# Sixteen conditioning rows at the start of a decoder kernel: summed by TensorE in column form instead of by VectorE

## The chip, the cores and the metric

The kernel runs on 1 core of one Trainium2 chip. The metric is the device time of one execution in microseconds (us), lower is better.

## The reference, cut to what matters

A two-layer decoder trunk on 256 tokens of width 1024. Every layer is steered by a conditioning vector: `mod = silu(c) @ w_mod + b_mod`, six rows of 1024 numbers a layer. The first two of them, shift and scale, are needed before anything else of the layer can be computed:

```python
c_act = jax.nn.silu(c)
for l in range(DEPTH):
    mod = (c_act @ w_mod[l] + b_mod[l])[:, None, :]
    sh1, sc1, g1, sh2, sc2, g2 = jnp.split(mod, 6, axis=-1)
    h = x * (1.0 + sc1) + sh1
    y = hybrid_mixer(h, w_in[l], ...)          # projections, sparse attention, gated linear attention
    x = layer_norm(DN_ALPHA * x + (1.0 + g1) * y, ...)
    h = x * (1.0 + sc2) + sh2
    y = swiglu(h, ...) if l % 2 == 0 else moe_swiglu(h, ...)
    x = layer_norm(DN_ALPHA * x + (1.0 + g2) * y, ...)
```

All of it is in f32.

## The kernel before

Every engine has its own program, and semaphores tie them together. The DMA queue of SyncE (SP) issues nearly all loads in an order that is written out by hand, and waits in that order too: what stands behind a waiting load waits with it.

The product `c_act @ w_mod[0]` for shift (a = 0) and scale (a = 1) is cut into sixteen blocks of 128 x 1024: block (a, k) holds the 128 input rows k of part a, so a row of the block lies on a partition. `FIRST_ROWS` is the order in which they are loaded: (1,0) to (1,3), then (1,4), (0,0), (1,5), (0,1), (1,6), (0,2), (1,7), (0,3), and last (0,4) to (0,7). The two halves of the tokens x are loaded behind the entries 9 and 11 of that list (`X_AFTER`). Below, block 0 to block 15 are the entries of this list.

VectorE takes each block as it lands, multiplies it by one number per partition (`c_act[:, k]`, silu of c, with the input index on the partitions) and adds it to the sum of its part, `ycat[:, a, :]` (lines 1464 and 1467). When a part is whole (`mod_sum`), TensorE sums over the partitions: `sum_chunk` (lines 1016 to 1019) multiplies eight pieces of 128 columns by a column of ones, so that the sums come out as eight columns, in the form in which VectorE needs them. Each piece is four matmuls of 128 x 32 weights (`mm4`, line 974), and each such f32 matmul is two matmul records and two weight loads in the trace. One part is thus 64 records.

In between, TensorE transposes a bias tile into bank 7 (`stage`, line 1013), waits until VectorE has copied it (`cols_rd`), transposes a second one (`stage2`, line 1024), and transposes the tokens (`transposed_tokens`, line 983: 16 transposes of 128 x 128 into banks 0 to 3). It does this between the sums of the two parts.

The sum of the second part signals `mod_ps`. Then:

- VectorE adds the biases (line 1454, `conditioning`) and modulates the transposed tokens, eight tiles of `hfull` (line 1499).
- TensorE starts unit 0 of the input projection (line 1054: f32, 32 records; a projection unit is 256 columns of `w_in`), then unit 1 (line 1048).
- ScalarE splits later units into a high part (line 679, `u_high`), VectorE makes the low part (line 1550, `u_low`), and TensorE multiplies them (lines 340 to 342). ScalarE's order is: split unit 2, high part of the tokens (line 720), split unit 3, copy the results of units 0 and 1 out (lines 701 and 705), split unit 4.
- SP, which has issued units 0 to 3 without a wait, issues conditioning rows 0 and 1 of the later parts into the buffers of `ycat`, behind `mod_ps` (line 412), then unit 4 behind the end of unit 0's matmuls (`proj`, line 427), for unit 4 takes its buffer. Rows 2 and 3 come next, behind VectorE's work on row 0, then unit 5.
- GpSimd, which had waited for `mod_sum` of both parts, issues the loads of `g_row`, `wa2`, `lng_row`, `lnb_row` and `gnorm` (lines 592 to 610).

The rest of the kernel: attention and gated linear attention of layer 0, a dense SwiGLU, the mixer of layer 1, and from about 540 us on the routed experts, TensorE's longest stretch.

Of the kernel before, what the change touches and what calls it, by code (L numbers as in the profile page):

```python
# [20 lines left out]
ALU = mybir.AluOpType  # L21
# [3 lines left out]
P = 128  # L25
D = 1024
KT = D // P
# [62 lines left out]

FIRST_ROWS = [(1, k) for k in range(4)] + [(a, k + 4 * a) for k in range(4) for a in (1, 0)] + [(0, k) for k in range(4, 8)]
X_AFTER = (9, 11)

HF0, HF1, YC0, YC1, X0 = range(5)
NROWBUF = X0 + 8
# [14 lines left out]
def hybrid_decoder(nc, x, c, w_in, w_a2, b_a, gla_norm_g, w_out, w_mod, b_mod, ln_g, ln_b,  # L110
# [3 lines left out]
    with ctx:  # L114
# [17 lines left out]
        x_sb = place("x_sb", [P, TT, D])  # L132
        hTH_at = top[0]
        hT_H = place("hT_H", [P, KT, T], F32R)
        hTL_at = top[0]
        hT_L = place("hT_L", [P, KT, T], F32R)
        hfull_at = top[0]
        hfull = place("hfull", [P, KT, T])
        ycat_at = top[0]
        ycat = place("ycat", [P, TT, D])  # L140
# [14 lines left out]
        ident = place("ident", [P, P])  # L155
# [5 lines left out]
        stage2 = place("stage2", [P, P])  # L161
        ln_cols = place("ln_cols", [P, 64])
        cols = place("cols", [P, P])
        modT = place("modT", [P, DEPTH * 48])
# [3 lines left out]
        c_act = place("c_act", [P, KT])  # L168
# [90 lines left out]
        mod_first = place("mod_first", [P, KT, 2 * D], at=over)  # L259
# [37 lines left out]
        bank = [ctx.enter_context(nc.psum_tensor(f"bank{i}", [P, 512], F32)) for i in range(8)]  # L297


        s = {}  # L300
        for name in """const c_ld x_ld stage_ld stage2_ld small_ld rows_ld wa2_ld pads stageT cols_rd cact mod_sum ik row_rd mod_ps modT x_ln xT_ps hfull hT_H hT_L
            brow_ld gn_ld wH wL proj evac idx_ps relu idxacc dve_chain act_chain pool_chain z_ps az decay
            qe ke kx_e kfac_rd gla_in hfull_a lnm wo at_ps at_sb at_msk o_ps ssq rms lg_ps lg_sb nmax pexp pt_ps pt_sb pv_ps ycat
            yT_ps yT_H yT_L mv rstd x_n g3 stored
            f_guH f_guL f_gu f_silu f_hid f_t f_tH f_tL f_dH f_dL f_d
            rt_ps lg8 expd sel rank_ps npass lg_rd xb_ps xsplit G xg_ps xg
            zeroed row_to sent x_rows x_turned y_kept y_all row_back came
            m_used m_silu m_hid m_tH m_oS m_st m_S m_sc m_acc m_y0 m_y1 m_end""".split():
            s[name] = sem("s_" + name)
        row_ld = [sem(f"s_row_ld{i}") for i in range(NROWBUF)]  # L310
        mod_ld = row_ld + [sem(f"s_mod_ld{i}") for i in range(NROWBUF, len(FIRST_ROWS))]
# [222 lines left out]
        def _(pool):  # L534
            n = [0]
# [80 lines left out]
                    link(pool.tensor_scalar(rms[:, t, :], ssq[:, t, :], 1.0 / B_DV, EPS, ALU.mult, ALU.add))  # L616
                    pool.tensor_tensor(rms[:, t, :], rms[:, t, :], half_neg[:, 4:8], ALU.pow).then_inc(s["rms"], 1)

            pool.wait_ge(s["mod_sum"], 2)
            gate_bias(0, 2, g_row)  # L620
            mixer(0)
            norm_power(0)
# [344 lines left out]
        def _(pe):  # L967
# [9 lines left out]
            def transposed_tokens(src, signal):  # L977

                for b in range(4):
                    for i in range(2):  # L980
                        for t in range(TT):
                            kt = 2 * b + i
                            last = nc.tensor.transpose(bank[b][:, i * T + t * P:i * T + (t + 1) * P],
                                                       src[:, t, kt * P:(kt + 1) * P], ident[:])
                    last.then_inc(s[signal], 1)
# [29 lines left out]
            def sum_chunk(acc, o):  # L1015

                for k in range(KT):
                    last = mm4(o[:, k:k + 1], acc[:, k * P:(k + 1) * P], ones[:, 0:1], start=True, stop=True)
                return last
            pe.wait_ge(s["mod_sum"], 1)  # L1020
            sum_chunk(ycat[:, 1, :], bank[6][:, KT:2 * KT])
            pe.wait_ge(s["cols_rd"], 1)
            pe.wait_ge(s["stage2_ld"], 32)
            nc.tensor.transpose(bank[7][:, 0:P], stage2[:], ident[:]).then_inc(s["stageT"], 1)
            pe.wait_ge(s["x_ld"], 32)
            transposed_tokens(x_sb, "xT_ps")
            pe.wait_ge(s["mod_sum"], 2)
            sum_chunk(ycat[:, 0, :], bank[6][:, 0:KT]).then_inc(s["mod_ps"], 1)

            def project(l, u, between=None):  # L1030
                b = bank[4 + u % 2]
# [303 lines left out]
            for t in range(TT):  # L1335
                for kt in KT_ORDER:
                    token_tile(3, t, kt)
                    last = mm4(bank[(7, 5)[t]][:, 0:NE], hfull[:, kt, t * P:(t + 1) * P], wr[:, kt, :],
                               start=(kt == KT_ORDER[0]), stop=(kt == KT_ORDER[-1]))
# [88 lines left out]
            for t in range(TT):  # L1428
                for g in range(GROUPS):
                    if t == 0:  # L1430
                        pe.wait_ge(s["m_y1"], n_done + g + 1)
                    for h in range(2):
                        half = slice(64 * h, 64 * h + 64)
                        last = mm(bank[(6, 0)[t] + h][:], last_S[half, g, t * P:(t + 1) * P], y_last[half, g, :],
                                  start=(g == 0), stop=(g == GROUPS - 1))
# [5 lines left out]
        def _(dve):  # L1441
            V = nc.vector
            n = [0]
# [11 lines left out]
                                              in1=cols[:, c0:c0 + 8], op0=ALU.add, op1=ALU.add)  # L1455


            dve.wait_ge(s["cact"], 1)
            before = [0, 0]
            for i, (a, k) in enumerate(FIRST_ROWS):  # L1460
                dve.wait_ge(mod_ld[i], 16)
                w, acc = mod_first[:, k, a * D:(a + 1) * D], ycat[:, a, :]
                if k == 0:
                    last = V.tensor_scalar(acc, w, c_act[:, 0:1], None, ALU.mult)
                else:
                    dve.wait_ge(s["dve_chain"], before[a])
                    last = V.scalar_tensor_tensor(out=acc, in0=w, scalar=c_act[:, k:k + 1], in1=acc,
                                                  op0=ALU.mult, op1=ALU.add)
                if k == KT - 1:
                    last.then_inc(s["mod_sum"], 1)  # L1470
                else:
                    last.then_inc(s["dve_chain"], 1)
                    n[0] += 1
                    before[a] = n[0]
                if i == 8:
                    dve.wait_ge(s["stageT"], 1)
                    V.tensor_copy(cols[:], bank[7][:, 0:P]).then_inc(s["cols_rd"], 1)
            dve.wait_ge(s["cols_rd"], 1)
            dve.wait_ge(s["mod_ps"], 1)
            for a in range(2):  # L1480
                last = conditioning(0, a, bank[6][:, a * KT:(a + 1) * KT])
# [354 lines left out]
            for t in range(TT):  # L1836
                last = V.tensor_tensor(lg[:, t, :], bank[(7, 5)[t]][:, 0:NE], br_row[:], ALU.add)
# [21 lines left out]
            for p in range(1, PASSES):  # L1859
                last = V.tensor_scalar(rank_tab[:, :, 1 + p * NE:1 + (p + 1) * NE], rank_m[:], -1.0 - p * SLOTS, None, ALU.add)  # L1860
# [25 lines left out]
            for p in range(PASSES):  # L1886
                last = V.tensor_tensor(gate_tab[:, :, 1 + p * NE:1 + (p + 1) * NE], gate[:], tmp[:], ALU.add)
# [90 lines left out]
            for t in range(TT):  # L1978
                last = V.tensor_scalar(last_G[:, t].rearrange("p g (q s) -> p g q s", q=4),
                                       slot_id[:, 0:SLOTS].rearrange("p (g s) -> p g s", g=GROUPS).unsqueeze(2).broadcast_to([P, GROUPS, 4, 32]),  # L1980
                                       rank_tab[:, t, bass.ds(n_done, 1)], None, ALU.is_equal)
            last.then_inc(s["m_oS"], 1)
            dve.wait_ge(s["came"], 32 * TT)
            for t in range(TT):
                link(V.tensor_scalar(ycat[:, t, :], back[t][0][:], gate_back[:, 0, t:t + 1], None, ALU.mult))
                link(V.scalar_tensor_tensor(out=ycat[:, t, :], in0=back[t][1][:], scalar=gate_back[:, 1, t:t + 1], in1=ycat[:, t, :],
                                            op0=ALU.mult, op1=ALU.add))
                link(V.tensor_tensor(ycat[:, t, :], ycat[:, t, :], gate3_row[:], ALU.mult))
                link(V.scalar_tensor_tensor(out=ycat[:, t, :], in0=x_sb[:, t, :], scalar=ALPHA, in1=ycat[:, t, :],
                                            op0=ALU.mult, op1=ALU.add))  # L1990
# [4 lines left out]
            for t in range(TT):  # L1995
                accumulate(n_done, (2 * t, 2 * t + 1), ((6, 7), (0, 1))[t])
                dve.wait_ge(s["m_acc"], 2 + 2 * t)
                for h in range(2):
                    last = V.bn_stats(stats[:, t, h, :], ycat[:, t, h * 512:(h + 1) * 512])
# [4 lines left out]
            for t in range(TT):  # L2004
                last = V.scalar_tensor_tensor(out=x_sb[:, t, :], in0=ycat[:, t, :], scalar=mv[:, t, 0:1], in1=lng_row[:],
                                              op0=ALU.subtract, op1=ALU.mult)
# [29 lines left out]
```

## Time and profile before

| | us |
|---|---|
| median of 3 runs | 1260.71 |
| lowest, highest | 1260.42, 1261.34 |
| profiled execution, its own time | 1262.0 |
| its span in the trace | 1260.3 |
| TensorE matmul busy | 1155.7 |
| VectorE busy | 546.0 |
| ScalarE busy | 284.0 |

The span runs from the first instruction to the last; the execution's own time is 1.7 us longer. Busy shares are over the whole span, and stages differ: in the first 125 us VectorE is busy most of the time and TensorE often waits, and in the last 700 us TensorE is nearly always busy.

### The profile page before, as it was taken

The numbers are of one execution on the slowest core, as the hardware profiler recorded it, in microseconds if no ns is written. First come the engines' busy times: TensorE is split into PE (matmuls) and PEld (weight loads), VectorE is DVE, ScalarE is ACT, GpSimd is POOL, SyncE is SP. The second block draws the span as 40 slices with busy tenths as digits, with TensorE's granted clock in tenths as the row PEclk, the third lists the DMA queues.
The fourth block names the chain that finished last, engine by engine and source line by source line (L and its number), as shares of the span: only waits on it lengthen the run. The fifth ranks groups of instructions, "written<-read, shape, count | busy, mean of one in ns | idle before, by whom it ended". The sixth has DMA issues, their size and how long they took to land.

```text
span 1260.3 us, 25818 instructions
## 1 busy us (share of the span) xinstructions
PE 1155.7 (92%) x11004; PEld 634.8 (50%) x11004; DVE 546.0 (43%) x881; ACT 284.0 (23%) x486; POOL 64.9 (5%) x118
## 2 busy tenths in 40 slices
PE   1887979999988899899999999999999999999986
PEld 1876868778867898642333333333333333333322
DVE  6798688867756999842110110121011101110124
ACT  0553524343334656211010010010000100100100
POOL 2102000000202001010000000000000000000101
PEclk9998989999989999899999999999999999999988
DMA  9979496889972955999999999999999999999991
GB/s 341 323 233 278 173 335 210 296 324 385 303 249 67 290 172 177 362 388 338 413 412 398 410 405 404 412 397 412 412 392 411 413 390 410 412 402 411 412 389 56
DMA packets 156504, 422.69 MB, mean 335 GB/s; under 512 B 20988, under 2 KB 74656, under 8 KB 145120
## 3 DMA queue, kind: packets, MB, share of 16 engines
q1 hardware_dynamic: 146720, 395.16, 82.3%
q0 software_dynamic: 6080, 20.31, 5.0%
q10 hardware_dynamic: 3584, 5.51, 1.3%
q8 instruction: 89, 1.46, 0.5%
q14 instruction: 31, 0.25, 0.1%
HBM read 405.20 MB, written 15.73 MB: 334 GB/s over the span
## 4 chain that ended last, share of the span: by engine, by line
PE 67%; DVE 13%; DMA 11%; issue 4%; SPq 3%; ACT 2%; POOL 0%; DVEq 0%; ACTq 0%
PE bank L1372 32%; PE bank L1386 17%; PE bank L340 4%; PE bank L342 4%; PE bank L341 4%; DMA raw_u<-in_ffn_w_up_dram 4%; DVE mod_acc L1539 3%; DMA raw_w<-in_moe_w_down_dram 3%; DVE u_low L1550 2%; DMA raw_w<-in_moe_w_up_dram 2%; DMA u_raw<-in_w_in_dram 1%; PE bank L1260 1%; DMA mod_first<-in_w_mod_dram 1%; SPq L487 1%; ACT gu_H L843 1%
## 5 line engine op out<-in xcount | busy, mean ns | idle before, releaser
L1372 PE MATMUL bank<-raw_w,xg 128*32 128x512 f32 (+1 forms) x4608 | 460.1, 558 | 5.2 <-DMA raw_w<-in_moe_w_up_dram 3.0
L1372 PEld LDWEIGHTS bank<-raw_w,xg 128*32 128x32 f32 x4608 | 154.0, 110 | 308.1 <-issue 300.5
L1924 DVE TENSOR_TENSOR he<-he,bank 128x256 f32<-128x256 f32 (+1 forms) x72 | 25.7, 384 | 533.8 <-ACT he L897 533.8
L1386 PE MATMUL bank<-raw_w,heT 128*32 128x512 f32 x2112 | 232.9, 596 | 3.0 <-DMA raw_w<-in_moe_w_down_dram 2.9
L1386 PEld LDWEIGHTS bank<-raw_w,heT 128*32 128x32 f32 x2112 | 71.9, 110 | 157.7 <-issue 152.9
L897 ACT ACTIVATE he<-bank 128x256 f32<-128x256 f32 (+1 forms) x72 | 21.3, 367 | 571.2 <-PE bank L1372 571.2
L1539 DVE SCALAR_TENSOR_TENSOR mod_acc<-mod_row,c_act,mod_acc 128x1024 f32<-128x1024 f32 x70 | 89.8, 1283 | 9.1 <-DMA mod_row<-in_w_mod_dram 3.2
L340 PE MATMUL bank<-u_high,hT_H 128*128 128x256 f32 x256 | 74.7, 292 | 4.7 <-DVE u_low L1550 3.3
L342 PE MATMUL bank<-u_high,hT_L 128*128 128x256 f32 x256 | 72.1, 282 | 0.0
L341 PE MATMUL bank<-u_low,hT_H 128*128 128x256 f32 x256 | 72.0, 281 | 0.0
L679 ACT ACTIVATE u_high<-u_raw 128x2048 fp32r<-128x2048 f32 x26 | 49.7, 1912 | 69.3 <-DMA u_raw<-in_w_in_dram 43.8
L340 PE MATMUL bank<-gu_H,hT_H 128*128 128x512 f32 x160 | 64.8, 405 | 0.0
L342 PE MATMUL bank<-gu_H,hT_L 128*128 128x512 f32 x160 | 63.2, 395 | 0.0
L341 PE MATMUL bank<-gu_L,hT_H 128*128 128x512 f32 x160 | 63.1, 394 | 0.0
L1550 DVE TENSOR_TENSOR u_low<-u_raw,u_high 128x2048 fp32r<-128x2048 f32 x26 | 59.2, 2286 | 4.1 <-ACT u_high L679 3.9
L1935 DVE TENSOR_TENSOR y_sum<-y_sum,bank 32x512 f32<-32x512 f32 x48 | 32.9, 686 | 46.2 <-ACT y_sum L912 45.1
L340 PE MATMUL bank<-hT_H,u_high 128*128 128x256 f32 x176 | 51.2, 291 | 1.8 <-DVE u_low L1548 1.8
L340 PEld LDWEIGHTS bank<-u_high,hT_H 128*128 128x128 f32 x256 | 48.2, 188 | 7.7 <-DVE u_low L1550 4.0
L342 PE MATMUL bank<-hT_H,u_low 128*128 128x256 f32 x176 | 49.9, 284 | 0.0
L341 PE MATMUL bank<-hT_L,u_high 128*128 128x256 f32 x176 | 49.9, 283 | 0.0
L341 PEld LDWEIGHTS bank<-u_low,hT_H 128*128 128x128 f32 x256 | 48.3, 189 | 0.7 <-issue 0.7
L342 PEld LDWEIGHTS bank<-u_high,hT_L 128*128 128x128 f32 x256 | 48.2, 188 | 0.0
(299 smaller groups left out, 1269.2 us busy)
## 6 DMA issues: line engine op xcount, KB each, us to landing
raw_w<-in_moe_w_down_dram SPq DMA_DIRECT2D x88, 1024.0 KB, 16.8
raw_w<-in_moe_w_gate_dram SPq DMA_DIRECT2D x128, 512.0 KB, 13.3
raw_w<-in_moe_w_up_dram SPq DMA_DIRECT2D x128, 512.0 KB, 15.7
mod_row<-in_w_mod_dram SPq DMA_DIRECT2D x80, 512.0 KB, 7.2
raw_w<-in_moe_w_gate_dram SPq DMA_DIRECT2D x64, 384.0 KB, 11.9
raw_w<-in_moe_w_up_dram SPq DMA_DIRECT2D x64, 384.0 KB, 13.6
u_raw<-in_w_in_dram SPq DMA_DIRECT2D x20, 1024.0 KB, 7.3
raw_d<-in_ffn_w_down_dram SPq DMA_DIRECT2D x11, 1024.0 KB, 10.7
```

Of the source, the lines that this page charges most:

```text
L340: nc.tensor.matmul(out_ap, aH, bH, start=first, stop=False)
L341: nc.tensor.matmul(out_ap, aH, bL, start=False, stop=False)
L342: return nc.tensor.matmul(out_ap, aL, bH, start=False, stop=last)
L487: sp.dma_start(raw_w[i][:, 1, 0:CHUNK_W[c]], mu[e, :, f].rearrange("(p b) f -> b p f", b=KT)[k]).then_inc(m_ld[i], 16)
L679: A(dst[:], src[:], ACT.Copy).then_inc(s["wH"], 1)
L897: A(he[:, g, 0:w].rearrange("s (j b c) -> s j b c", b=2, c=32), bank[g][:, 0:w].rearrange("s (j c b) -> s j b c", b=2, c=32), ACT.Silu).th ...
L1372: last = mm(bank[g][32 * q:32 * q + 32, 0:2 * HALF[c]].rearrange("s (m j r) -> s m j r", m=2, r=64), xg[:, i, g, k, :], cols[:, :, :, 64 * ...
L1386: last = mm(bank[3 + g][32 * q:32 * q + 32, :], heT[(par + c) % 2][:, g, 2 * a + b, :], W[:, b, h * 512:(h + 1) * 512], start=(c == 0 and ...
L1539: last = V.scalar_tensor_tensor(out=acc, in0=row[:], scalar=c_act[:, k:k + 1], in1=acc, op0=ALU.mult, op1=ALU.add)
L1550: V.tensor_tensor(L[:], src[:], H[:].bitcast(F32), ALU.subtract).then_inc(s["wL"], 1)
L1924: V.tensor_tensor(h, h, bank[g][:, w:2 * w].rearrange("s (j c b) -> s j b c", b=2, c=32), ALU.mult).then_inc(s["m_hid"], 1)
L1935: last = V.tensor_tensor(a, a, bank[3 + g][64 * h + 32:64 * h + 64, :], ALU.add)
```

## The change

The sixteen blocks go to TensorE. For each block, as it lands, it makes the products of the eight pieces of 128 columns with the column `c_act[:, k]` (instead of a column of ones), and adds them up in bank 6, where each of the sixteen columns takes eight blocks. VectorE's two lines, its sums in `ycat` and the signal `mod_sum` go. The transposes of the second bias tile and of the tokens stand behind block 13 (`TOKENS_AFTER`). VectorE copies the first bias tile at once. GpSimd waits for `mod_ps` instead of `mod_sum`.

```diff
+TOKENS_AFTER = 13
...
-            pool.wait_ge(s["mod_sum"], 2)
+            pool.wait_ge(s["mod_ps"], 1)
...
-            pe.wait_ge(s["mod_sum"], 1)
-            sum_chunk(ycat[:, 1, :], bank[6][:, KT:2 * KT])
-            pe.wait_ge(s["cols_rd"], 1)
-            pe.wait_ge(s["stage2_ld"], 32)
-            nc.tensor.transpose(bank[7][:, 0:P], stage2[:], ident[:]).then_inc(s["stageT"], 1)
-            pe.wait_ge(s["x_ld"], 32)
-            transposed_tokens(x_sb, "xT_ps")
-            pe.wait_ge(s["mod_sum"], 2)
-            sum_chunk(ycat[:, 0, :], bank[6][:, 0:KT]).then_inc(s["mod_ps"], 1)
+            pe.wait_ge(s["cact"], 1)
+            for i, (a, k) in enumerate(FIRST_ROWS):
+                pe.wait_ge(mod_ld[i], 16)
+                for j in range(KT):
+                    first = a * D + j * P
+                    last = mm4(bank[6][:, a * KT + j:a * KT + j + 1], mod_first[:, k, first:first + P], c_act[:, k:k + 1],
+                               start=(i == 0 and j == 0), stop=(i == 2 * KT - 1 and j == KT - 1))
+                if i == TOKENS_AFTER:
+                    pe.wait_ge(s["cols_rd"], 1)
+                    pe.wait_ge(s["stage2_ld"], 32)
+                    nc.tensor.transpose(bank[7][:, 0:P], stage2[:], ident[:]).then_inc(s["stageT"], 1)
+                    pe.wait_ge(s["x_ld"], 32)
+                    transposed_tokens(x_sb, "xT_ps")
+            last.then_inc(s["mod_ps"], 1)
...
+            dve.wait_ge(s["stageT"], 1)
+            V.tensor_copy(cols[:], bank[7][:, 0:P]).then_inc(s["cols_rd"], 1)
             dve.wait_ge(s["cact"], 1)
-            before = [0, 0]
-            for i, (a, k) in enumerate(FIRST_ROWS):
-                dve.wait_ge(mod_ld[i], 16)
-                w, acc = mod_first[:, k, a * D:(a + 1) * D], ycat[:, a, :]
-                if k == 0:
-                    last = V.tensor_scalar(acc, w, c_act[:, 0:1], None, ALU.mult)
-                else:
-                    dve.wait_ge(s["dve_chain"], before[a])
-                    last = V.scalar_tensor_tensor(out=acc, in0=w, scalar=c_act[:, k:k + 1], in1=acc,
-                                                  op0=ALU.mult, op1=ALU.add)
...
-                if i == 8:
-                    dve.wait_ge(s["stageT"], 1)
-                    V.tensor_copy(cols[:], bank[7][:, 0:P]).then_inc(s["cols_rd"], 1)
```

## Rows read from the trace of the kernel before

**Rows 1.** The page: busy time of the engines, chain that ended last by engine

```profile
PE 1155.7 (92%) x11004; PEld 634.8 (50%) x11004; DVE 546.0 (43%) x881; ACT 284.0 (23%) x486; POOL 64.9 (5%) x118
...
PE 67%; DVE 13%; DMA 11%; issue 4%; SPq 3%; ACT 2%; POOL 0%; DVEq 0%; ACTq 0%
```

**Rows 2.** Chain that ended last, 0 to 50 us: start, duration, what

```profile
9.88 15.36 DMA mod_first<-in_w_mod_dram
...
30.77 1.08 PE bank L974 x64
...
31.95 0.25 DVE modT L1454 x2
...
32.92 9.47 PE bank L1054 x32
...
42.41 6.39 DMA u_raw<-in_w_in_dram
```

**Rows 3.** Timeline of VectorE, 6 to 125 us: start, duration, idle before

```profile
21.48 2.56 DVE L1467 SCALAR_TENSOR_TENSOR ycat<-mod_first,c_act,ycat 128x1024 f32<-128x1024 f32 x2 [1.11 <-DMA mod_first<-in_w_mod_dram]
25.27 5.45 DVE L1467 SCALAR_TENSOR_TENSOR ycat<-mod_first,c_act,ycat 128x1024 f32<-128x1024 f32 x4 [1.23 <-DMA mod_first<-in_w_mod_dram]
...
45.16 2.29 DVE L1550 TENSOR_TENSOR u_low<-u_raw,u_high 128x2048 fp32r<-128x2048 f32 x1 [1.63 <-ACT u_high L679]
...
50.77 2.29 DVE L1550 TENSOR_TENSOR u_low<-u_raw,u_high 128x2048 fp32r<-128x2048 f32 x1 [1.25 <-ACT u_high L679]
...
122.00 2.29 DVE L1550 TENSOR_TENSOR u_low<-u_raw,u_high 128x2048 fp32r<-128x2048 f32 x1 [1.05 <-ACT u_high L679]
```

**Rows 4.** VectorE's waits, 32 to 125 us: for whom, total, times, longest

```profile
DVE u_low L1550 <- ACT u_high L679: 3.9, 3, 1.6
...
DVE prob L1665 <- PE bank L1106: 0.6, 1, 0.6
```

**Rows 5.** Timelines of TensorE: start, duration, what

```profile
8.64 0.48 PE L1013 MATMUL bank<-ident,stage 128*128 128x128 f32 x1 [8.64 <-POOL half_neg L565]
22.82 1.03 PE L974 MATMUL bank<-ones,ycat 128*32 128x1 f32 x64 [13.71 <-DVE ycat L1467]
23.79 0.48 PE L1024 MATMUL bank<-ident,stage 128*128 128x128 f32 x1
...
24.06 3.54 PE L983 MATMUL bank<-ident,x_sb 128*128 128x128 f32 x16
...
67.67 2.21 PE L974 MATMUL bank<-u_raw,hfull 128*32 128x72 f32 x128
...
140.24 1.97 PE L1122 MATMUL bank<-ident,ycat 128*128 128x128 f32 x16 [2.07 <-DVE ycat L1736]
...
537.24 0.25 PE L974 MATMUL bank<-rt,upper 128*32 128x8 f32 x8 [0.61 <-DVE rt L1850]
```

**Rows 6.** Stretches: length, PE, PEld, DVE, ACT, POOL busy (instructions), granted clock, DMA share, GB/s

```profile
31.00:32.00 1.00, 0.80 (x61) 0.72 (x56) 0.05 (x1) 0.00 (x0) 0.89 (x2) 0.50 1.24 295
...
37.00:38.00 1.00, 1.00 (x5) 0.85 (x4) 0.00 (x0) 1.00 (x2) 0.10 (x1) 0.69 1.11 341
...
47.00:48.00 1.00, 1.00 (x11) 1.00 (x10) 1.00 (x2) 0.00 (x0) 0.00 (x0) 1.00 0.49 159
...
529.20:532.60 3.40, 3.14 (x74) 2.81 (x75) 1.16 (x4) 1.62 (x5) 0.00 (x0) 0.50 1.02 405
```

**Rows 7.** The token transposes (line 983), 27 to 28 us: shortest, median, longest in ns

```profile
L983 PE MATMUL bank<-ident,x_sb x4: 324/417/417, 26.6 to 27.3; 128*128 128x128 f32 x4
```

**Rows 8.** Timelines of GpSimd and ScalarE, 30 to 50 us

```profile
31.01 0.57 POOL L592 DMA_DIRECT2D g_row<-in_b_mod_dram  x1 [20.48 <-DVE ycat L1467]
...
43.15 1.91 ACT L679 ACTIVATE u_high<-u_raw 128x2048 fp32r<-128x2048 f32 x1 [3.40 <-DMA u_raw<-in_w_in_dram]
44.97 0.58 ACT L701 ACTIVATE bqT<-bank 128x512 f32<-128x512 f32 x1
```

**Rows 9.** Timeline of TensorE's weight loads at unit 0

```profile
32.88 9.09 PEld L1054 LDWEIGHTS bank<-hfull,u_raw 128*128 128x128 f32 x32 [1.17 <-DMA u_raw<-in_w_in_dram]
```

More of the change, by code:

```diff
@@ L300, in hybrid_decoder @@
         s = {}
-        for name in """const c_ld x_ld stage_ld stage2_ld small_ld rows_ld wa2_ld pads stageT cols_rd cact mod_sum ik row_rd mod_ps modT x_ln xT_ps hfull hT_H hT_L
+        for name in """const c_ld x_ld stage_ld stage2_ld small_ld rows_ld wa2_ld pads stageT cols_rd cact ik row_rd mod_ps modT x_ln xT_ps hfull hT_H hT_L
             brow_ld gn_ld wH wL proj evac idx_ps relu idxacc dve_chain act_chain pool_chain z_ps az decay
@@ L1455, in conditioning @@
                                               in1=cols[:, c0:c0 + 8], op0=ALU.add, op1=ALU.add)
+            dve.wait_ge(s["stageT"], 1)
+            V.tensor_copy(cols[:], bank[7][:, 0:P]).then_inc(s["cols_rd"], 1)
             dve.wait_ge(s["cact"], 1)
-            before = [0, 0]
-            for i, (a, k) in enumerate(FIRST_ROWS):
-                dve.wait_ge(mod_ld[i], 16)
-                w, acc = mod_first[:, k, a * D:(a + 1) * D], ycat[:, a, :]
-                if k == 0:
-                    last = V.tensor_scalar(acc, w, c_act[:, 0:1], None, ALU.mult)
-                else:
-                    dve.wait_ge(s["dve_chain"], before[a])
-                    last = V.scalar_tensor_tensor(out=acc, in0=w, scalar=c_act[:, k:k + 1], in1=acc,
-                                                  op0=ALU.mult, op1=ALU.add)
[L1469 to L1474, printed above, removed]
-                if i == 8:
-                    dve.wait_ge(s["stageT"], 1)
-                    V.tensor_copy(cols[:], bank[7][:, 0:P]).then_inc(s["cols_rd"], 1)
             dve.wait_ge(s["cols_rd"], 1)
```

## The prediction

> **What bounds the kernel now.** I read the page first: TensorE leads the chain that ended last with 67% of the span, VectorE has 13%, DMA 11% [rows 1]. That is a mean over stages, and the change touches only the first 32 us, so I read the chain there. It waits for the blocks to land (15.36 us to 25.24), runs through VectorE's last four blocks, then through the column sums (30.77 to 31.85), the bias add at 31.95, unit 0's matmuls (32.92 to 42.39) and the load of unit 4, which may only start when they end and lands 6.39 us later, at 48.80 [rows 2]. So the start is bound by DMA up to block 12 and by VectorE after it: the blocks 12 to 15 took 5.45 us without a pause, 1.36 each, while the transfers come faster. From the wait that ended at 21.48 (block 10) to the one that ended at 25.27 (block 12) three transfers of 512 KB landed (block 11, half of x, block 12) in 3.79 us, 1.26 each [rows 3]. Block 13 is thus due at about 26.5, 14 at 27.8, 15 at 29.1, and VectorE ends at 30.72.
>
> Next I asked what is worth what after `mod_ps`. VectorE splits unit 4 at 50.77 after an idle wait of 1.25 us. From there to 120 us it waits for other engines only 0.6 us (its next wait for a split, 1.05, ends at 122) [rows 3, 4]. So VectorE bounds the mixer from 50.77 on, and a shift of that instant shifts the rest. What sets it is unit 4's landing, and through it the end of unit 0's matmuls. `mod_ps` itself counts only as far as it moves that end.
>
> **The change part by part.**
>
> *VectorE's sixteen blocks and the sum over partitions go.* On the path this removes block 15's tail on VectorE (29.1 to 30.72) and the last 64 matmul records (1.08 us). The blocks of VectorE before it lie beside the transfers and are worth nothing; VectorE has no other work that could move up.
>
> *TensorE gets sixteen runs of 64 small records.* Such a run took 1.03 us [rows 5], 16 ns a record; 128 records with 72 columns took 2.21 us, 17 ns a record. A block lands every 1.26 us, so by the rows TensorE keeps up: it starts at 9.1 (after the transpose at 8.64), works off blocks 0 to 5 back to back by about 15.3, and then waits for each block. Block 13 lands at 26.5 and is done at 27.6.
>
> *The transposes move behind block 13.* They waited for nobody before: from 23.79 to 27.60 TensorE did them while VectorE was still adding, 3.81 us hidden [rows 5]. Now they stand in TensorE's queue in front of the last two blocks, which lie landed from 27.8 and 29.1 on. At the same pace they end at 27.6 + 3.8 = 31.4, the two blocks take 2.1, and `mod_ps` comes at 33.5 instead of 31.85, 1.65 us later. The cover that VectorE's adds gave to the transposes is gone, and this costs more than the removed tail.
>
> *The clock decides how much of it comes back.* The view by stretches gives a granted clock of 0.50 (1.2 GHz) at 31:32, after TensorE had been idle for 3.2 us, and 0.69 at 37:38, that is, back to 1.00 (2.4 GHz) at about 37.7 [rows 6]. Unit 0 thus ran 4.8 us of its 9.47 at half speed; at 2.4 GHz throughout it would take 4.8/2 + 4.7 = 7.1. Ahead of the first change the view shows 1.00 without proof: the token transposes took 417 ns and the last one 324 [rows 7], and their 16 took 3.54 us where 16 others took 1.97 at 140 us [rows 5]. So they ran at 1.2 GHz and the clock rose at their end. In the changed kernel the pause between the small records and unit 0 is only 1.07 us (31.85 to 32.92 before). If the clock rises during the transposes, as it did, and holds over this pause, unit 0 runs from 33.5 + 1.07 = 34.6 to 41.7, 0.7 earlier than before. If it doesn't hold or rise, unit 0 takes 9.5 again and ends at 44.1, 1.7 later. The rows don't tell which: between both ends lies the uncertainty, and I take the middle, 42.9, 0.5 later.
>
> The Trainium skill has a rule that speaks against the first end. "TensorE: Matmul & The Clock Gate", Part 4 (PE-mode transpose), says that transposes do not lift the clock. By it unit 0 would always start at half speed and the sum would be +1.7. The 324 ns behind the 417 ns, and a view that shows a fall at all, disagree with it here.
>
> *GpSimd waits for `mod_ps`.* Its loads started at 31.01 [rows 8] and now start at about 33.6. None is late: the first user of `wa2` is the decay product behind ScalarE's copies, which start at 44.97 [rows 8], 11 us on; the rows for the layer norm are wanted only at the end of the mixer. But they share the DMA engines with units 2 to 4; bounds for that are 0 and a rival below. SP's rows 0 and 1 move by the same 1.65 us; VectorE takes them from 47.4 on, behind unit 3's split of 45.16 + 2.29, which leaves room.
>
> *What else hangs on unit 0's end.* ScalarE copies its result at 44.97, behind unit 3's split [rows 8], so an end up to 44.1 delays nothing there. VectorE's and ScalarE's work on the tokens stands behind unit 2's split and has over 1 us of slack (VectorE waited 1.63 before unit 3's split [rows 3]).
>
> *Unit 4.* Its issue moves with unit 0's end, by -0.7 to +1.7. Its landing follows less when earlier: the DMA share at 47:48 is 0.49 [rows 6], so only about half a microsecond of transfer room stands empty ahead of the landing, and VectorE, busy until 49.52, can gain 1.25 at most. Later it follows in full. So the kernel moves by between -0.5 and +1.7. Sum at the middle: +0.5 on the span of 1260.3, 1260.8; the execution's own time is 1.7 above its span and 1.3 above the median of 1260.71. I set the shift on the median: 1261.2. What a measurement of this kernel can tell from no change is about 0.2%, 2.5 us, and all of this lies inside.
>
> **The rivals.**
>
> *Small matmuls wake the clock.* If the stream from 9 us on lifts it before the transposes, these take 2.2 (0.27 and 1.97) and end at 29.8, `mod_ps` comes at 31.9, unit 0 starts at 33.0 (it can hardly start earlier: its own weights landed at 32.88 [rows 9]) and ends at 40.1, 2.3 earlier. With the cap on unit 4's landing the gain is 0.5 to 1.25, so 1259.8. Against it: at 529.2:532.6 TensorE was busy for 3.14 of 3.40 us with transposes and 64 small records, and the clock stayed at 0.50 [rows 6]. Chance 0.13.
>
> *GpSimd's later loads let unit 3 land earlier.* ScalarE waited 3.40 us until 43.15 for unit 3 [rows 8], while GpSimd's rows were in flight. Without them in front, the split of unit 3 starts up to 3.4 earlier, and VectorE's 1.63 and TensorE's start on unit 2 come forward; unit 4's landing still caps the gain. About 1.3 us, 1259.4. Chance 0.10.
>
> *TensorE doesn't keep up* (the slower side). The point is 1.26 us / 64 = 19.7 ns a record; from there each further ns costs 16 x 64 ns = 1.0 us on `mod_ps`, and beyond 1.7 us all of it passes on. In favour: eight records alone took 0.25 us, 31 ns each [rows 5], no row shows more than 128 in a row, and every run now begins with a wait. Against: 16 and 17 ns in the runs of 64 and 128. At 31 ns it would be 12 us; I price it at 24 ns, midway between 17 and 31, which makes +5, 1266. Chance 0.12.
>
> Of this the Trainium skill has a figure: "TensorE: Matmul & The Clock Gate" (Wait — 56ns, not 53.3ns?) gives 25 ns start to start as the floor for a matmul however small. By it the sum would be about +6. The rows' 16 ns disagree.
>
> *The forecast*, -0.5 to +1.7: 0.65.
>
> **How the numbers follow.** Time 1261.2. The forecast's own range is 1260.2 to 1262.4, widened by 1 us each way for scatter of runs (1260.42 to 1261.34 before) and for the gaining rivals below: 1259.2 to 1263.4 leaves out most of the third rival (0.12) and some tails. Faster by over 0.2%: 0.04, for no case reaches 2.5 us alone. Slower: 0.13, the third rival and a little of the forecast's late end. Same: 0.83.
>
> **What would show it.** Runs of 64 on line 974 at about 1.03 us, each starting where a block lands, up to 27.6; transposes from 27.6 to 31.4 and `mod_ps` at 33.5 (bias add on VectorE at 33.6); unit 0 from 34.6, with the granted clock 1.00 or 0.50 deciding between 41.7 and 44.1; unit 4's split on VectorE at 50.3 to 52.5; from there a constant shift. I am wrong if small records take over 20 ns, if the clock is full before 27 us, if unit 3's split starts well ahead of 43.15, or if the kernel moves by more than VectorE's instant at 50.77 does.

## The result and the profile after

The changed kernel takes 1276.36 us (median of 4 runs, 1270.84 to 1280.61) where the kernel before takes 1261.03 (4 runs, 1260.42 to 1263.43): ratio 1.0129, 95% interval 1.0081 to 1.0177. It is slower by about 15 us, where 1261.2 had been forecast. The profiled execution took 1272.97, its span is 1271.2 (before: 1262.0 and 1260.3).

The page of the changed kernel, its head and its instruction queue:

```profile
span 1271.2 us, 27580 instructions
...
PE 1166.4 (92%) x11900; PEld 648.9 (51%) x11900; DVE 526.6 (41%) x865; ACT 284.4 (22%) x486; POOL 64.2 (5%) x118
...
q8 instruction: 96, 1.57, 0.5%
```

and the same queue on the page of the kernel before:

```profile
q8 instruction: 89, 1.46, 0.5%
```

VectorE lost 19 us of busy time, as intended, and TensorE got 896 matmul records and 896 weight loads more (11900 against 11004 each). That is 1792 instructions, and the queue that brings instructions moved 7 packets more, of 16 KB each: 256 instructions a packet. The columns of that row are packets, MB and share of the DMA engines. It is the row that I had not looked at.

The timeline of TensorE in the changed kernel, 8 to 58 us (start, duration, what; the idle time before it and what ended it in brackets). It answers to [rows 5] and to the TensorE steps of [rows 2]:

```profile
...
8.60 3.15 PE L975 MATMUL bank<-c_act,mod_first 128*32 128x1 f32 x221
15.69 1.88 PE L975 MATMUL bank<-c_act,mod_first 128*32 128x1 f32 x128 [3.94 <-issue]
21.89 1.89 PE L975 MATMUL bank<-c_act,mod_first 128*32 128x1 f32 x128 [4.32 <-issue]
27.82 1.88 PE L975 MATMUL bank<-c_act,mod_first 128*32 128x1 f32 x128 [4.04 <-issue]
33.75 1.89 PE L975 MATMUL bank<-c_act,mod_first 128*32 128x1 f32 x128 [4.05 <-issue]
39.41 1.88 PE L975 MATMUL bank<-c_act,mod_first 128*32 128x1 f32 x128 [3.77 <-issue]
43.42 0.70 PE L975 MATMUL bank<-c_act,mod_first 128*32 128x1 f32 x35 [2.13 <-issue]
...
44.32 3.62 PE L984 MATMUL bank<-ident,x_sb 128*128 128x128 f32 x16
47.87 1.47 PE L975 MATMUL bank<-c_act,mod_first 128*32 128x1 f32 x128
50.48 7.23 PE L1060 MATMUL bank<-hfull,u_raw 128*128 128x256 f32 x32 [1.14 <-DVE hfull L1488]
```

Three things are to be seen. The records themselves run at the pace that I had read, 128 in 1.88 us, 15 ns each. They come in portions of 128, which with their 128 weight loads are 256 instructions, and not in the portions of 64 that a block has. And ahead of each portion TensorE stops for "issue", that is, for nothing that the profile shows as a wait: about 4 us five times, 2.13 the sixth. From 15.69 to 39.41 a portion starts every 5.93 us on average (15.69, 21.89, 27.82, 33.75, 39.41), so a record costs 46 ns, not 16, against 19.7 at which TensorE keeps up with the landings. The name "issue" alone proves nothing: the kernel before has one such wait too, of 8.5 us at line 1177. It is the counting, and the runs below, that tie these stops to the supply of instructions. TensorE's waits over the stretch 8 to 50 us sum the stops up (total, times, longest):

```profile
PE bank L975 <- issue: 22.2, 6, 4.3
```

VectorE's timeline in the changed kernel, which answers to [rows 3], and the stretch 35 to 50 us by the engines, with granted clock, DMA share and GB/s last:

```profile
49.51 0.24 DVE L1460 SCALAR_TENSOR_TENSOR modT<-bank,cols 128x8 f32<-128x8 f32 x2 [40.52 <-PE bank L975]
...
65.99 2.29 DVE L1539 TENSOR_TENSOR u_low<-u_raw,u_high 128x2048 fp32r<-128x2048 f32 x1 [3.42 <-ACT u_high L680]
```

```profile
35.00:40.00 5.00, 1.23 (x92) 1.14 (x92) 0.00 (x0) 1.91 (x1) 0.00 (x0) 1.00 0.55 194
40.00:45.00 5.00, 2.87 (x138) 2.78 (x132) 0.00 (x0) 0.00 (x0) 0.00 (x0) 1.00 0.03 7
45.00:50.00 5.00, 4.34 (x142) 3.92 (x140) 0.45 (x3) 0.00 (x0) 0.34 (x1) 1.00 0.00 0
```

The bias add comes at 49.51 instead of 31.95, 17.6 us later. The blocks had all landed long before, and from 40 us on the DMA engines all but stand still (share 0.03, then 0.00). Unit 0 then runs at the full clock and takes 7.23 us where it took 9.47 [rows 2], which gives 2.2 back; it ends 15.3 later (57.71 against 42.39), and the split of unit 4 starts 15.2 later (65.99 against 50.77). The spans differ by 10.9 us. About 2.5 of the difference came back in the dense SwiGLU, where TensorE's longest wait at 300 to 400 us is shorter; kernel before, then changed kernel:

```profile
PE bank L340 <- DVE d_L L1778: 5.3, 1, 5.3
```

```profile
PE bank L341 <- DVE d_L L1767: 2.8, 1, 2.8
```

### The profile page after: what moved, and what is told of

Its sections match the earlier page's. It is cut to its first block, busy times and chain, and to the rows that moved or that the text cites. A ratio compares the mean times of both kernels' runs of the same rounds, so it can differ in the third digit from the quotient of the medians.

```text
span 1271.2 us, 27580 instructions
## 1 busy us (share of the span) xinstructions
PE 1166.4 (92%) x11900; PEld 648.9 (51%) x11900; DVE 526.6 (41%) x865; ACT 284.4 (22%) x486; POOL 64.2 (5%) x118
## 4 chain that ended last, share of the span: by engine, by line
PE 60%; DMA 7%; DVE 7%; issue 1%; ACT 1%; SPq 1%; POOL 0%; DVEq 0%; ACTq 0%
PE bank L1378 32%; PE bank L1392 18%; DMA raw_w<-in_moe_w_down_dram 4%; PE bank L341 3%; PE bank L343 3%; PE bank L342 3%; DMA raw_u<-in_ffn_w_up_dram 2%; DVE u_low L1539 1%; DMA u_raw<-in_w_in_dram 1%; DVE mod_acc L1528 1%; PE bank L1367 1%; DVE score L1583 0%; ACT gu_H L844 0%; PE bank L975 0%; SPq L497 0%
## 5 line engine op out<-in xcount | busy, mean ns | idle before, releaser
L342 PE MATMUL bank<-hT_L,u_high 128*128 128x256 f32 x176 | 49.5, 281 | 0.0
(297 smaller groups left out, 1271.2 us busy)
## 6 DMA issues: line engine op xcount, KB each, us to landing
raw_d<-in_ffn_w_down_dram SPq DMA_DIRECT2D x11, 1024.0 KB, 10.9
```

The source lines that it names most:

```text
L342: nc.tensor.matmul(out_ap, aH, bL, start=False, stop=False)
```

## The experiments

Two theories stood against each other. **Fetch**: TensorE uses up its instructions faster than they are brought. **Pace**: small matmuls that wait for a landing, read a tile into which DMA writes beside them, or add into one bank are slow by themselves. "Bias add" below is the start of VectorE's line 1454 (31.95 in the kernel before).

**The changed kernel again.** 

> The changed kernel once more, nothing altered, because its four times spread over 10 us. Two theories. Fetch: TensorE runs out of instructions; after about 440 instructions of the small matmuls it gets 256 at a time (128 small matmul records and their weight loads), every 5.9 us while the loads run and about every 4 us when they are quiet. Expects stops of 3.8 to 4.4 us after each 128 records again, not at block borders, the bias add near 49.5 us (47 to 58, since a fetch's delay may vary from run to run), 1271 to 1281. Pace: small matmuls that wait for a landing, read a tile that DMA writes beside them, or add into one bank are slow by themselves. Expects stops that follow the blocks of 64 records, not multiples of 128 records, and little spread.

Measured: 1274.02 us (4 runs, 1272.68 to 1275.91) against 1258.4 for the kernel before on the same chip, ratio 1.0131 (1.0097 to 1.0166). Stops of 3.55, 4.32, 4.32, 4.05, 3.77 and 1.58 us, again ahead of portions of 128 records (the last again ahead of 35 and the transposes); bias add at 48.63. Its span was 1273.0; in this execution the wait in the dense SwiGLU was 4.8 us, not 2.8. So the stops repeat within 0.6 us. That part of the spread between runs comes from what later stages give back is suggested by these two executions, not shown. Unit 0 did not repeat: it took 8.83 us here, not 7.23, and the granted clock fell during it (same columns as [rows 6]):

```profile
49.60 8.83 PE L1060 MATMUL bank<-hfull,u_raw 128*128 128x256 f32 x32 [1.14 <-DVE hfull L1488]
```

```profile
51.00:52.00 1.00, 1.00 (x4) 0.82 (x3) 1.00 (x3) 0.90 (x1) 1.00 (x3) 0.50 0.98 373
```

**As many instructions, no work.**

```diff
+            for i in range(112):
+                mm4(bank[5][:, 0:1], ident[:], ones[:, 0:1], start=True, stop=True)
```

> The kernel before, with 448 small matmuls (896 records) put into TensorE's program behind the first transpose: no waits, constant operands, each result overwritten, nothing reads them. As many instructions as the change adds. Fetch: stops of about 4 us after every 128 records from about the 220th on, the extra ones end near 44 us instead of 24, the bias add comes at 46 to 50 instead of 31.95, 1270 to 1281 us. Pace (waits, landing data, accumulation): 16 ns a record, they end at 9 + 14.6 = 23.7, the sums lose at most 1 us, 1260.5 to 1262.

Measured: 1273.7 us (4 runs) against 1258.4, ratio 1.0134 (1.0096 to 1.0172). TensorE's timeline of this kernel:

```profile
9.00 3.16 PE L974 MATMUL bank<-ones,ident 128*32 128x1 f32 x222
16.12 1.89 PE L974 MATMUL bank<-ones,ident 128*32 128x1 f32 x128 [3.96 <-issue]
22.04 1.89 PE L974 MATMUL bank<-ones,ident 128*32 128x1 f32 x128 [4.04 <-issue]
...
39.81 1.89 PE L974 MATMUL bank<-ones,ident 128*32 128x1 f32 x128 [4.03 <-issue]
44.36 0.64 PE L974 MATMUL bank<-ones,ident 128*32 128x1 f32 x33 [2.67 <-issue]
```

The same picture, record for record, with no waits, constant operands and no sums: the first stop after 222 records instead of 221, then one after every 128. Bias add at 50.83. The pace theory falls: VectorE still does its sixteen blocks here, and the kernel is as slow as the changed one.

**The same work as a loop.**

```diff
+            with nc.Fori(0, 14, engines=[pe.engine], hint_back_edge=True):
+                for i in range(8):
+                    mm4(bank[5][:, 0:1], ident[:], ones[:, 0:1], start=True, stop=True)
```

> The same 448 small matmuls as a hardware loop of 14 turns of 32, so the same work in 1/14 of the instructions. Fetch: no stops (128 instructions and their branch can stay where they are), they end at 24 to 27 us, bias add at 32 to 33, 1260.5 to 1262.5. If instead the engine can't sustain so many small matmuls by themselves: stops as in the straight-line version, 1270 or more.

Measured, TensorE's timeline:

```profile
9.02 15.60 PE L974 MATMUL bank<-ones,ident 128*32 128x1 f32 x896
24.46 1.03 PE L974 MATMUL bank<-ones,ycat 128*32 128x1 f32 x64
...
30.85 1.03 PE L974 MATMUL bank<-ones,ycat 128*32 128x1 f32 x64 [1.54 <-DVE ycat L1470]
```

896 records in 15.60 us without a stop, bias add at 32.03. So it is not the number of small matmuls but the number of instructions that must be brought. The transposes behind them took as long as ever (shortest, median and longest in ns):

```profile
L983 PE MATMUL bank<-ident,x_sb x16: 417/418/418, 25.7 to 28.9; 128*128 128x128 f32 x16
```

The time, however, was 1263.19 (10 runs) against 1258.4, ratio 1.0033 (1.0009 to 1.0056), above what I expected. TensorE's waits at 700 to 1000 us, in the routed experts, show where it went:

```profile
PE bank L1375 <- issue: 7.5, 3, 3.6
```

The kernel before has no wait of this kind there. Its expert loop is the same code, 128 instructions and a loop further back in the program. The runs below follow this up.

**Half of the blocks on TensorE.** TensorE takes the eight blocks of the shift part directly, VectorE the others:

```diff
+ON_PE = [i for i, (a, k) in enumerate(FIRST_ROWS) if a == 0][-8:]
...
+            def direct(i):
+                a, k = FIRST_ROWS[i]
+                pe.wait_ge(mod_ld[i], 16)
+                for j in range(KT):
+                    last = mm4(bank[5][:, j:j + 1], mod_first[:, k, j * P:(j + 1) * P], c_act[:, k:k + 1],
+                               start=(i == ON_PE[0] and j == 0), stop=(i == ON_PE[-1] and j == KT - 1))
+                return last
```

> VectorE keeps the eight blocks of the scale part; TensorE sums the eight blocks of the shift part directly (into bank 5). The transposes stand where they stood before the change. 1188 instructions ahead of the bias add instead of 2230. Fetch: 512 run at once, the other 680 need three more fetches of 256, of which the last two bind: bias add at 36 to 40, 1264 to 1270. Pace per block: the change's 17.5 us over 16 blocks, so half of it, 8.7: bias add at 41, or, if only the waits of the last four blocks count, at 33 to 34 and 1262. The positions of the stops tell them apart: every 128 records or at each block.

Measured: 1267.77 us (9 runs) against 1258.4, ratio 1.0073 (1.0052 to 1.0094); bias add at 36.72. The last stretch of TensorE's timeline:

```profile
29.20 0.29 PE L975 MATMUL bank<-c_act,mod_first 128*32 128x1 f32 x12
29.99 1.25 PE L975 MATMUL bank<-c_act,mod_first 128*32 128x1 f32 x128 [0.49 <-issue]
34.82 1.77 PE L975 MATMUL bank<-c_act,mod_first 128*32 128x1 f32 x116 [3.59 <-issue]
```

The early blocks lie far enough apart for the instructions to follow; the last four don't, and the stops come after 12 and 128 records, inside blocks. Counted from the start of the program, 700 matmuls and weight loads lie ahead of the first of these stops (first transpose 2, four blocks 512, column sums 128, transposes 2 + 32, 12 records 24) and 956 ahead of the second: 444, where the changed kernel stops first, and once and twice 256 more. The bias add is 4.8 us later than before. Of the 9.4 us by the medians another part belongs to stops in the experts, 7.7 us in all (last section).

**Two blocks, and one.** The edge should lie where TensorE has used up what it had at the start. VectorE gives up its last two blocks, or its last one, and TensorE adds them to the column sums:

```diff
+ON_PE = [i for i, (a, k) in enumerate(FIRST_ROWS) if a == 0][-2:]    # or [-1:]
...
+            for j in range(KT):
+                mm4(bank[5][:, j:j + 1], ycat[:, 0, j * P:(j + 1) * P], ones[:, 0:1], start=(j == 0), stop=False)
+            for i in ON_PE:
+                last = direct(i)
+            last.then_inc(s["mod_ps"], 1)
```

> VectorE keeps all blocks but the last two (14 and 15); TensorE takes their products directly, added to the column sums in bank 5; transposes as before the change. Some 550 instructions ahead of the bias add. Fetch: the changed kernel ran 443 instructions of small matmuls before its first stop, here the 292nd stands at 29 us, so TensorE stops once, inside block 15, until about 33 to 34.5: bias add at 33 to 35. Pace: no stop, bias add at 31.2 (28.0 + 3 x 1.03 and a hop).

> The same with the last block alone (15) on TensorE: some 420 instructions ahead of the bias add, fewer than the 443. Fetch: no stop of the 4 us kind, bias add at 31.5 to 31.7, and unit 0 starts no earlier than before, for its weights land at about 32.9. Pace: the same number here. Together with the run with two blocks it places the edge. In the routed experts: 128 instructions more than before the change (half a fetch), so stops of about 3.5 us at two or three turns of the expert loop, as in the run with the small loop, if the place of the loop in the program is their cause.

Measured, TensorE with two blocks:

```profile
29.19 1.21 PE L975 MATMUL bank<-c_act,mod_first 128*32 128x1 f32 x76
33.95 0.91 PE L975 MATMUL bank<-c_act,mod_first 128*32 128x1 f32 x52 [3.55 <-issue]
```

It stops for 3.55 us after 76 records of the two blocks, bias add at 34.98. Counted in matmuls and weight loads, that is 2 + 128 + 2 + 32 + 128 + 152 = 444 instructions from the start of the program (bias transpose, column sums of part 1, second bias transpose, token transposes, column sums, 76 records with their weight loads); in the changed kernel it is 2 + 221 x 2 = 444, in the run without work 2 + 222 x 2 = 446. With one block no stop occurs at the start, and the bias add comes at 30.70, 1.25 earlier than before and 0.8 earlier than I had written. It is worth next to nothing: unit 0 waits for its weights and starts only 0.8 us earlier,

```profile
32.11 9.62 PE L1066 MATMUL bank<-hfull,u_raw 128*128 128x256 f32 x32 [1.52 <-DMA u_raw<-in_w_in_dram]
```

and the split of unit 4 starts at 50.69, against 50.77 before. One run each: 1267.12 with two blocks, 1261.49 with one, before 1260.25 (median of 15). With two blocks the split of unit 4 starts only 1.6 us later (52.35); where the rest of the 6.9 us arose was not followed up, and it is one run. The kernel with one block also has the stops in the experts, as expected (waits of TensorE at 700 to 1000 us):

```profile
PE bank L1384 <- issue: 7.6, 4, 3.3
```

**Only a pad.** Eight `mm4` (128 instructions) behind the first transpose, otherwise the kernel before.

> The kernel before with 32 idle small matmuls (128 instructions) behind the first transpose, nothing else. Two runs with an odd multiple of 128 instructions more showed stops of 3.4 to 3.6 us of TensorE at the start of turns of the expert loop near 745 and 924 us. If they come from where the loop lies against the 256-instruction pieces: the start of the kernel is unchanged (bias add at 31.9 to 32.1), and these stops are there; median 2 to 6 us above before. If they came from the additional loop or from the direct sums: no stops and no change.

Measured: 1263.89 us (6 runs) against 1260.25, ratio 1.0032 (1.0016 to 1.0049). Bias add at 32.53, half a microsecond later than I expected (VectorE's blocks ended that much later). TensorE at the start of two turns of the expert loop:

```profile
742.03 1.92 PE L1374 MATMUL bank<-raw_w,xg 128*32 128x512 f32 x15 [0.58 <-issue]
747.45 21.20 PE L1374 MATMUL bank<-raw_w,xg 128*32 128x512 f32 x177 [3.50 <-issue]
918.38 1.92 PE L1374 MATMUL bank<-raw_w,xg 128*32 128x512 f32 x15 [0.32 <-issue]
923.58 19.50 PE L1374 MATMUL bank<-raw_w,xg 128*32 128x512 f32 x177 [3.28 <-issue]
```

15 records into a turn TensorE has nothing to issue for 3.3 to 3.5 us. 128 idle instructions 730 us earlier suffice for this. The page of this kernel shows more than the pad on the instruction queue:

```profile
q8 instruction: 92, 1.51, 0.5%
```

That is 3 packets more than before for half a packet of instructions. The kernels with 256 instructions more (two direct blocks, and the next run) move one more, those with 1792 more move seven.

**One block, and an even pad.** The kernel with one direct block again, and eight idle `mm4` more where TensorE waits for ScalarE anyway, so that the program is 256 instructions longer than before the change.

```diff
+                if l == 0:
+                    for i in range(8):
+                        mm4(bank[6][:, 0:1], ident[:], ones[:, 0:1], start=True, stop=True)
                 pe.wait_ge(s["evac"], l * NIN + U_BA + 1)
```

> The version with the last block alone on TensorE, and 32 idle small matmuls (128 instructions) more where TensorE waits for ScalarE behind unit 1 anyway, so that the program is 256 instructions longer than before the change instead of 128. If the stops at the turns of the expert loop (7.6 us in the version without them) come from where the loop lies against the 256-instruction pieces: they are gone, only waits for DMA remain there as before the change. Bias add at 30.7 to 31.6 as in the version without. Kernel 1257.5 to 1261 where before is about 1260, that is, from 2.5 faster to no difference, for the earlier bias add is worth nothing while unit 0's weights land at 32 to 33. If the stops stay, their cause is the direct block, not the place.

Measured: 1259.0 us (12 runs) against 1259.15, ratio 0.9997 (0.9983 to 1.0011). No wait for issue is left in the experts; bias add at 31.20. So these stops come from the place of the loop, and the version is as fast as the kernel before, not faster.

**Wider weights.** The obvious repair: the same products with a quarter of the instructions.

```diff
-                    last = mm4(bank[6][:, a * KT + j:a * KT + j + 1], mod_first[:, k, first:first + P], c_act[:, k:k + 1],
+                    last = mm(bank[6][:, a * KT + j:a * KT + j + 1], mod_first[:, k, first:first + P], c_act[:, k:k + 1],
```

> The changed kernel with full 128 x 128 weights instead of four pieces of 128 x 32: a quarter of the instructions (about 550 ahead of the bias add), same products. Fetch: no row of stops of 4 us, one at most; but a weight load of 128 columns takes 190 to 226 ns instead of the 16 ns pace of four at a time, so a block takes 3.0 to 3.6 us instead of 1.03, TensorE is bound by that from the start, the bias add comes at 60 to 70 and the kernel at 1280 to 1300. If the loads of wide weights overlap better than that: blocks at 1.7 to 2.1 us, bias add at 40 to 46. If stops of about 4 us come every 128 records here too, fetch isn't the cause of those in the changed kernel.

Measured: 1289.33 us (one run; before 1259.15). TensorE's timeline:

```profile
8.46 47.79 PE L1026 MATMUL bank<-c_act,mod_first 128*128 128x1 f32 x224
```

No stop, but 213 ns a record: 3.4 us a block, and the bias add at 66.75. At this pace 256 instructions last 27 us, so they are brought in time, and the pace itself is the bound.

**Keeping the clock up.** The prediction had found half of unit 0 at 1.2 GHz. In the kernel before, four idle f32 matmuls of 256 columns follow the token transposes:

```diff
             transposed_tokens(x_sb, "xT_ps")
+            for i in range(4):
+                mm(bank[5][:, 0:T], ident[:], ones[:], start=True, stop=True)
             pe.wait_ge(s["mod_sum"], 2)
```

> The kernel before with four idle f32 matmuls of 256 columns (16 instructions) behind the token transposes, so that TensorE is not idle for 3.2 us ahead of the last column sums. They take 1.7 us at the full clock. If the half clock during unit 0 comes from this pause: granted clock 1.00 through unit 0, which takes 7.1 instead of 9.5 and ends near 40.1 instead of 42.4; unit 4's split on VectorE starts 0.5 to 1.25 earlier (49.5 to 50.3), the kernel gains as much. If unit 4's landing is bound by transfers alone: the split stays at 50.8 and nothing is gained.

Measured: 1262.19 us (10 runs) against 1260.25, ratio 1.0009 (0.9997 to 1.0021). Stretches (same columns as [rows 6]):

```profile
32.00:34.00 2.00, 0.63 (x9) 0.53 (x4) 1.77 (x6) 0.00 (x0) 1.71 (x5) 1.00 1.12 344
34.00:36.00 2.00, 2.00 (x8) 1.65 (x7) 2.00 (x5) 0.00 (x0) 2.00 (x4) 0.67 1.06 364
36.00:38.00 2.00, 2.00 (x6) 1.53 (x6) 0.17 (x1) 0.00 (x0) 1.65 (x4) 0.50 1.06 367
```

The granted clock held until about 34.7 and then fell all the same, with 1.5 us of idling, 0.7 of small records, 1.4 of idling and 1.3 us of unit 0 behind it; the 64 small records took 0.71 us instead of 1.03, unit 0 took 8.86 us instead of 9.47 and started half a microsecond later. Unit 4's split began at 50.89, unchanged. The first half of the expectation failed, so the second was not put to the test.

## Why the prediction was wrong, step by step

- **What bounds the start** (landings, then VectorE's adds, then the column sums): nothing in the runs speaks against it. With one block fewer on VectorE the bias add came 1.25 us earlier, and unit 0 then waited for its weights, as the prediction's first rival had it from [rows 9].
- **"So by the rows TensorE keeps up"**: this step failed. The pace of a record was right (15 ns) but was measured on runs of 64 and 128 records. What limits sixteen such runs in a row is the supply of instructions, 256 for 128 records every 5.93 us, 46 ns a record. After 444 matmuls and weight loads TensorE lives on what is brought. The run without work showed the same stops at the same counts, the loop showed none, and the versions with 16, 8, 2 and 1 direct blocks put the bias add at 49.5, 36.7, 35.0 and 30.7.
- **The rival "TensorE doesn't keep up"** had the right side and a point of decision, 19.7 ns, that stands. Its price was midway between two rows of short runs, 24 ns, and so +5; at 46 ns its own rule (1.0 us for each ns above 19.7) would have given about +26 on the bias add, where 17.6 was measured: the first 221 records ran at 15 ns, the sixth stop was only 2.13 us, and ahead of the last 128 there was none. It had 0.12, for no row shows more than 128 records in a row; that gap was named and then taken for evidence of no trouble.
- **The transposes behind block 13, +1.65**: not seen by itself. In the changed kernel they gave the instructions time to follow: the 128 records behind them start with the transposes' end, at 47.87, and run without a stop. No run tried another place.
- **The clock**: both ends were seen in two executions of the same kernel. In the first unit 0 ran at 1.00 throughout and took 7.23 us, predicted 7.1 for this end; in the repeat the clock was at 0.50 (1.2 GHz) from about 50.2 to 53.6 us and unit 0 took 8.83, though TensorE had had the same instructions ahead of it and idled the same 1.14 us. In the run without work it took 8.72. That the clock rose around the transposes fits the small records: 128 took 1.88 us ahead of them and 1.47 behind them (1.24 in the repeat). What decides whether it holds stays open.
- **The rival "Small matmuls wake the clock"** fell: in the loop 960 small records ran for over 16 us without a pause, and the transposes behind them still took 417 to 418 ns each. The rival on GpSimd's loads was not put to the test: in the changed kernel the units landed long before the small records ended.
- **The 25 ns that the Trainium skill gives as the floor of a matmul** ("TensorE: Matmul & The Clock Gate", Wait — 56ns, not 53.3ns?) would have given +6, nearer to the result but for another reason: the pace within a portion stayed at 15 ns.
- **From unit 0's end to unit 4's split**: the prediction had an earlier end capped at 1.25 us and a later one passed on in full. The end moved by -0.7 us with one direct block, +2.7 with two, +4.9 with eight and +15.3 in the changed kernel; the split of unit 4 moved by -0.1, +1.6, +3.7 and +15.2. So the gain was even smaller than its cap, and with two and eight blocks a delay lost 1.1 to 1.2 us on the way.
- **From there to the end**: that the rest of the kernel passes the shift on unchanged did not hold. VectorE's split at 122.00 came 14.1 later, the experts' run of 192 records that starts at 571.31 before 10.9 later, and from there on the shift stayed within 0.3. About 2.5 of what came back lies in the dense SwiGLU. In the repeat the same run of records came 15.0 later and the spans differed by 12.7. Why the stages give back different amounts was not tested.

The Trainium skill has the mechanism on the page "Runtime: NRT & Kernel Launch" (Instruction fetch mechanics): instructions come in blocks of 16 KiB, 256 of them, over a DMA queue that each engine drives itself, and a taken branch to a block that isn't there stops the engine. The traces agree on the size of a block (7 packets of 16 KB for 1792 instructions). On the branch they agree in part: stops of 3.3 to 3.6 us came behind two turns of the expert loop, but only in programs longer by an odd multiple of 128 instructions, and 13 to 15 records into the turn where the trace shows any records ahead of the stop. The page also holds that TensorE has room for 2048 instructions and that crossing a block is mostly hidden. Here TensorE stopped after 444 matmuls and weight loads and then for about 4 us ahead of each block as long as the loads ran, so this part doesn't hold for these runs.

## What to carry to other kernels

Count instructions, not only busy time: an engine that is fed many tiny operations can run dry though each of them is fast and the DMA engines are idle. Here an f32 product of 128 x 128 by one column became 16 instructions; whatever moves such work to TensorE at the start of a program was cheap here for the first 440 matmuls and weight loads of the program and cost 46 ns a record afterwards, unless a loop repeated them or pauses lay between them. A run of short operations in the trace of before shows the pace of a burst and not that of a stream, and the packets of the instruction queue are the row to read beside it.

## What the runs showed of the hardware

- TensorE got 256 instructions every 5.6 to 6.2 us while the loads ran (changed kernel, repeat, run without work). With the loads over it was faster: in the changed kernel the portion at 43.42 came 4.0 us after the one at 39.41, behind a stop of 2.13 us, with a DMA share of 0.03 at 40 to 45 us; in the repeat 3.5 us after, behind a stop of 1.58. How much of this is the loads is not settled, for with eight direct blocks one portion came after 4.8 us at full load (29.99 and 34.82).
- TensorE's small records have two paces: 64 in 1.03 us or 128 in 1.88, and 64 in 0.71 (behind the idle f32 matmuls) or 128 in 1.24 us (behind the transposes, in the repeat). The 15 to 16 ns read before the change is the slower one.
- The place of a loop in the program matters. Four kernels whose programs were longer than before by about an odd multiple of 128 instructions (the pad, the small loop, one direct block, eight direct blocks) stopped at two turns of the expert loop, 7.5 to 7.7 us in all in each; with 256 more (one block and the even pad, or two direct blocks) there was no such stop. The pad alone cost 0.32% (0.16 to 0.49), 3.6 us by the medians, less than the stops. In the profiled execution waits for DMA near the end are missing in exchange: TensorE's waits behind 1050 us in the kernel before were

```profile
PE bank L1372 <- DMA raw_w<-in_moe_w_up_dram: 3.0, 2, 2.3
PE bank L1386 <- DMA raw_w<-in_moe_w_down_dram: 2.9, 1, 2.9
```

and in the padded kernel only the last one, for VectorE's `y_last` (0.8 us), was left. From the experts' run of 192 records that starts at 571.31 before and at 569.54 with the pad, to the end, the padded kernel lost 2.2 us. An estimate of why half a block of 256 matters: the experts' records take 108 ns each (192 in 20.8 us), so 64 of them, 128 instructions, last 6.9 us, longer than the stops of 3.3 to 3.6 us; a turn that has so many more instructions at hand may hide its fetch. No trace shows where the blocks' borders lie. The change itself is 1792 instructions longer, seven times 256, and has none of these stops.
